# A run-through that orders the engines' steps, with eight numbers of its durations changed

## The reference

```
def peer(xn, wq, k1, k2, u_tab, v_tab):          # 8 heads, 128 x 128 experts
    q = xn @ wq                                   # two halves of 128 per head
    v1, i1 = top_k(q1 . k1, 16); v2, i2 = top_k(q2 . k2, 16)
    sv, ci = top_k(v1[:, None] + v2[None, :], 16) # 16 experts per head and token
    experts = e1 * 128 + e2                       # 128 per token
    hid = gelu(einsum("td,tkd->tk", xn, u_tab[experts]))
    return einsum("tk,tkd->td", softmax(sv) * hid, v_tab[experts])
```

## Time and profile before

| | |
|---|---|
| time, median of 3 runs | 2053.2 us (2052.7 to 2058.16) |
| the profiled execution's own time | 2048.43 us |
| its span, first to last instruction | 2046.6 us |
| TensorE's mean granted clock | 0.914 of 2.4 GHz |
| busy: PE, DVE, ACT, POOL | 81%, 69%, 40%, 30% |
| moved by DMA | 770.09 MB, mean 376 GB/s |

### The profile page before, as it was taken

How to read it: one execution, slowest core, us unless ns; L and a number is a source line. 1 busy time by engine, 2 the same in 40 slices (tenths; PEclk the granted TensorE clock), 3 DMA queues, 4 the chain that set the end, 5 groups by cost and what they waited for, 6 DMA issues and landing times.

```text
span 2046.6 us, 20781 instructions
## 1 busy us (share of the span) xinstructions
PE 1666.4 (81%) x6676; PEld 963.3 (47%) x6676; DVE 1406.5 (69%) x3607; ACT 817.2 (40%) x2072; POOL 610.9 (30%) x516
## 2 busy tenths in 40 slices
PE   8999989998889888886778877876887887756555
PEld 4449856583477464472326434532553463221111
DVE  4324327468776478866887876888887688877776
ACT  2423213433488236423444553333455324432222
POOL 0000000021422324523443343244425324454542
PEclk9999989899989999898889889988998899887878
DMA  9686868469999999999999999999999999999997
GB/s 391 211 312 237 298 227 279 170 222 388 386 419 419 420 418 407 420 418 407 420 420 419 419 419 420 399 420 420 419 420 412 416 354 419 419 420 420 421 420 306
DMA packets 108382, 770.09 MB, mean 376 GB/s; under 512 B 12144, under 2 KB 12656, under 8 KB 16368
## 3 DMA queue, kind: packets, MB, share of 16 engines
q0 software_dynamic: 73728, 536.90, 63.7%
q1 hardware_dynamic: 34544, 231.85, 29.4%
HBM read 767.65 MB, written 1.05 MB: 376 GB/s over the span
## 4 chain that ended last, share of the span: by engine, by line
PE 39%; DMA 37%; DVE 10%; issue 8%; ACT 3%; POOL 3%; SPq 0%; DVEq 0%; POOLq 0%
DMA arena<-in_peer_dram,eidx 10%; DMA ring<-in_peer_dram,eidx 10%; PE psum L1109 9%; DMA ring<-in_slabs_dram 9%; PE psum L745 8%; PE psum L768 8%; PE psum L954 6%; DMA kv<-in_peer_dram,eidx 5%; DMA early<-in_peer_dram,eidx 3%; PE psum L971 3%; DVE x L2023 2%; DVE arena L2013 1%; POOL arena L2165 1%; POOL ring L2165 1%; PE psum L786 1%
## 5 line engine op out<-in xcount | busy, mean ns | idle before, releaser
L2165 POOL DMA_INDIRECT arena<-in_peer_dram,eidx x203 | 244.8, 1206 | 832.5 <-DVE eidx L1885 440.2
L1109 PE MATMUL psum<-arena,diag 128*128 128x512 f32 x548 | 307.5, 694 | 109.1 <-ACT diag L1441 108.6
L1431 ACT ACTIVATE wexp<-wexp 128x1 f32<-128x1 f32 x512 | 103.2, 202 | 676.2 <-DVE wexp L2013 674.5
L2013 DVE CUSTOM_DVE_ANT_0 arena<-arena,osb 128x1024 f32<-128x1024 f32 x203 | 247.0, 1221 | 79.6 <-DMA arena<-in_peer_dram,eidx 76.8
L1109 PE MATMUL psum<-ring,diag 128*128 128x512 f32 x428 | 225.8, 661 | 61.4 <-ACT diag L1441 60.8
L2165 POOL DMA_INDIRECT ring<-in_peer_dram,eidx x155 | 185.0, 1193 | 295.8 <-PE psum L1109 234.3
L745 PE MATMUL psum<-ring,hT 128*128 128x512 f32 x560 | 258.6, 613 | 16.7 <-DMA ring<-in_slabs_dram 14.6
L1109 PEld LDWEIGHTS psum<-arena,diag 128*128 128x128 f32 x548 | 111.7, 216 | 269.6 <-ACT diag L1441 160.2
L2013 DVE CUSTOM_DVE_ANT_0 ring<-ring,osb 128x1024 f32<-128x1024 f32 x155 | 188.4, 1221 | 58.9 <-DMA ring<-in_peer_dram,eidx 57.0
L1109 PE MATMUL psum<-kv,diag 128*128 128x512 f32 x284 | 158.8, 688 | 53.3 <-ACT diag L1441 52.9
L954 PE MATMUL psum<-hT,ring 128*128 128x130 f32 x1408 | 168.0, 282 | 12.6 <-DMA ring<-in_slabs_dram 11.8
(11 more groups left out here) (328 smaller groups left out, 2131.0 us busy)
## 6 DMA issues: line engine op xcount, KB each, us to landing
ring<-in_slabs_dram SPq DMA_DIRECT2D x200, 1024.0 KB, 4.9
ring<-in_slabs_dram SPq DMA_DIRECT2D x8, 768.0 KB, 4.1
kept<-in_slabs_dram SPq DMA_DIRECT2D x4, 1024.0 KB
arena<-in_peer_dram,eidx POOLq DMA_INDIRECT x203
ring<-in_peer_dram,eidx POOLq DMA_INDIRECT x155
ring<-in_slabs_dram SPq DMA_DIRECT2D x4, 512.0 KB
kk<-in_keys_dram SPq DMA_DIRECT2D x2, 1024.0 KB, 8.9
kv<-in_peer_dram,eidx POOLq DMA_INDIRECT x105
```

The source lines that it names most:

```text
L1109: ins = pe.matmul(bank(b), diags_of(n), pair(slot_of[n])[:, 1024 + 512 * h:1536 + 512 * h], start=(k == 0), stop=(k == 127))
L1431: act.activation(wn, wn, ACT.Gelu_apprx_tanh).then_inc(*up("gelu", n))
L2013: v.tensor_tensor_reduce(out=row, in0=row, in1=row_y[t], scale=1.0, scalar=0.0, op0=ALU.mult, op1=ALU.add, accum_out=wexp[:, c:c + 1]).the ...
L2165: pool.indirect_dma_start(pair(i), None, tables, bass.IndirectOffsetOnAxis(ap=eidx[:, 128 * t + k:128 * t + k + 1], axis=0)).then_inc(sig. ...
```

## The change

Eight numbers of the run-through are set lower: the durations of a dot, a weight, a down on PE and a down on DVE, the floor and the constant part of a matmul's, and the constant parts of those of DVE's instructions.

```
-... T_DOT, T_WEIGHT, T_DIAG, T_TENSOR, T_VECTOR ... = ... 1.35, 0.55, 0.42, 2.1, 1.35 ...
+... T_DOT, T_WEIGHT, T_DIAG, T_TENSOR, T_VECTOR ... = ... 1.16, 0.52, 0.42, 1.8, 1.21 ...
     def matmul(self, out, lhsT, rhs, **k):
-        return self.run(max(0.232, 0.02 + 0.00166 * wide(rhs)) * (0.75 if lhsT.shape[0] <= 64 else 1.0))
+        return self.run(max(0.225, 0.01 + 0.00166 * wide(rhs)) * (0.75 if lhsT.shape[0] <= 64 else 1.0))
...
     def _vector(self, out, src, *a, **k):
-        return self.run(0.2 + 0.00107 * max(wide(out), wide(src)))
+        return self.run(0.12 + 0.00107 * max(wide(out), wide(src)))
...
     def tensor_tensor_reduce(self, out, in0, **k):
-        return self.run(0.28 + 0.00107 * wide(in0))
+        return self.run(0.2 + 0.00107 * wide(in0))
```

More of the change, by code:

```diff
@@ L29 @@
 ADD = ((0, 2), (6, 7), (0, 1), (6, 7))
-T_MB, T_SEEN, T_ISSUE, T_DOT, T_WEIGHT, T_DIAG, T_TENSOR, T_VECTOR, T_TABLE, T_HOP, T_KEEP, T_LEAN, T_AHEAD, T_LATE, T_PACE, T_SHRINK, T_FLIGHT, T_END, T_HEAD, T_FRESH, T_SCARCE, T_SOON, T_QUERY, T_ATT = 2.5, 2.0, 1.15, 1.35, 0.55, 0.42, 2.1, 1.35, 1.28, 0.12, 6, -2.0, 14, 0.0, 3.0, 0, 8, 0, 20, 0.5, 0, 10, 57, 62
+T_MB, T_SEEN, T_ISSUE, T_DOT, T_WEIGHT, T_DIAG, T_TENSOR, T_VECTOR, T_TABLE, T_HOP, T_KEEP, T_LEAN, T_AHEAD, T_LATE, T_PACE, T_SHRINK, T_FLIGHT, T_END, T_HEAD, T_FRESH, T_SCARCE, T_SOON, T_QUERY, T_ATT = 2.5, 2.0, 1.15, 1.16, 0.52, 0.42, 1.8, 1.21, 1.28, 0.12, 6, -2.0, 14, 0.0, 3.0, 0, 8, 0, 20, 0.5, 0, 10, 57, 62
 ENGINES = ("PE", "DVE", "ACT")
```

## The result

The changed kernel takes 2067.53 us (median of 4 runs, 2064.74 to 2070.72). The kernel before took 2054.71 us (2052.7 to 2058.16) in the runs beside it. The ratio is 1.0066, 95% interval 1.0046 to 1.0086: the change makes the kernel about 13 us slower. The prediction said 2048 us with a range of 2036 to 2064; the measured time lies outside of it. The profiled execution took 2070.72 us, its span is 2068.6. Three executions of the kernels with halved instructions further down, at 2581 to 2920 us, were in a slow state and are left out of every number.

A forecast was written before the change was run, and what follows sets the result against it. DMA, full at 420 GB/s, was taken as the bound. Terms of -6.7 us (440 to 530) and +1.5 (530 to 1660), the others 0, gave -5.2: 2053.2 to 2048 us, range 2036 to 2064.

The forecast's parts named there:

- What bounds the kernel: Whole span: DMA, full at 420 GB/s, needs 1833.5 of 2046.6 us; in the other 213 us it was not filled.
- Part 1: 0 to 440 us, up to the first gather: order swaps change nothing, 0, with 3 us to either side.
- Part 2: 440 to 530 us: earlier gathers close the 7.7 us hole, -6.7 us; between 0 and at most 12 of gain.
- the 8 us that I had named: Sign for 470 to 530 us: POOL never waits over 8 us there after the change.
- Part 3: 530 to 1660 us: stages packed into fewer pairs raise PE's share to 0.91; +1.5 us, bounds -16.7 and +24.
- M11's hole: End of M11, near 1500 us: the old hole of 8.1 us stays, some 150 us earlier, at 6 to 10 us.
- "about 18 us" of queue: Gather's issue to landing near the end: 20.52 us, transfer 2.5; a down may be about 18 us late before DMA notices.
- PE late in the stages: Rival: ends of M01 and M10 get holes of 8.1 us each, +9.5, 2063; 2071 if M11's doubles; chance 0.13.
- Its sign: Pairs 40 to 80, end of B1 and start of M01: a stretch with PE over 95% busy and DMA under 400.
- Part 4: Fourth tile, some 190 pairs with nearly all downs on PE: 2.44 us each, under 2.5 a pair, so 0.
- the rival of a PE alone at a low clock: Last 190 pairs: downs average over 2.5 us and every pair lags; +18 us, 2066 or 2071; chance 0.10.
- Part 5: The end: the last two downs stay on PE at 3.94 us; 0, at worst +3.6.

The follow-up runs named there:

- Halved dots: Changed kernel, same streams, each dot over 512 of its 1024 columns: 2045.21 us; the same edit in the kernel before: 2050.36 us.
- halved downs: Changed kernel, same streams, each down on PE one matmul instead of two except a tile's first and last: 2061.36 and 2057.69 us in two runs.
- the versions with a margin: Changed kernel with DVE's constants back at 0.2 and 0.28: 2041.23 us; with T_KEEP 8 for 6: 2040.18 us; with both: 2040.57 us.
- T_KEEP at 8: Changed kernel, T_KEEP 8 for 6, so dots and downs go ahead of steps with two pairs fewer landed: 2040.18 us, ratio 0.9942.

## Why the prediction was wrong, step by step

**What bounds the kernel** held: DMA at 420 GB/s, and each loss is time in which it was not filled. The sum over stretches closes within 1 us for both kernels.

**Part 1**, no change up to the first gather, was off by more than its own bound of 3 us: the first gather begins at 434.83 us, not 440.62, which is more than the 5 us that I had named as a sign of being wrong, and the stretch to 440 gained 3.1 us. I had counted the instructions ahead of it and taken a swap of single steps for nothing.

**Part 2** was right in place and sign, with a gain of 10.3 for 6.7. The hole of 7.7 us shrank to 1.8 (401 GB/s), the ramp before it from 4.9 to 0.6, which I had as the outer bound only. The downs of PE after the first came within 1 us of where I had put them (472.01 to 498.76), but 20 gathers were issued by 500 us, where I worked out 24 and before had 15. POOL waited twice for longer than the 8 us that I had named, 8.57 us before 474 and 13.23 before 515. The second wait follows 17.8 us of DVE without a dot, which looks like the mechanism of part 3 in small.

**Part 3 is the step that failed**: "I take +1.5 for the denser packing", bounds -16.7 and +24; it was +35.9. M11's hole, named at 6 to 10 us, was 19.7. The working behind it counted PE's share of each 20 to 40 pairs against DMA's and found 0.91 at most. DVE's was never counted. Its cover of "about 18 us" of queue was taken for a late down and put beside PE's work alone, though a late dot delays the same place. In fact the same packing that shortened the stages put DVE's searches, index arithmetic and mixers among fewer pairs: L rose from 11, 9 and 13 us in M01, M10 and M11 to 21, 20 and 20. Halved dots, which take work from DVE alone, give 22 us back. The row was there to see the earlier trace rows: DVE was busy 27.27 and 27.99 of 30 us at 1300 and 1660, the two stretches of before that had a hole, and PE 22.48 and 24.30. I read them for their GB/s and named PE from POOL's waits.

The rival "PE late in the stages" (0.13) had the right stages, M01 and M10, and a time near the measured one, 2063 to 2071. Its reason, "it decides where PE's share passes 1", holds for neither M10 nor M11: halved downs leave those holes nearly as they are. For M01 it was partly right. Its sign, pairs 40 to 80 with PE over 95% busy and DMA under 400 GB/s, came for 20 us (19.51 of 20 busy, 330 GB/s, at pairs 66 to 70), and halved downs take half of that hole away. M01's hole is not at that stage's end, where the rival had it, but in its middle.

**Part 4** was right. The 340 us from 1690 on stay at 420 GB/s, and the rival of a PE alone at a low clock fell. One line of PE's timeline and one stretch of the changed kernel near the end:

```profile
1934.10 1.98 PE L1109 MATMUL psum<-arena,diag 128*128 128x512 f32 x4 [0.51 <-ACT diag L1441]
```

```profile
1900.00:2000.00 100.00, 78.23 (x159) 1.00 1.01 420
```

Every down takes 1.98 us at a granted clock of 1.00, with gaps of 0.51 us, as the forecast had it (0.5 us, over 0.85). Before, it was 58.73 us for 20 downs at 0.74; now 78.23 for 40. The reading behind it was looser than it sounded: of the downs in the earlier trace rows the slowest, 3.78 us, follows 1.21 us of idle time and not 3. The Trainium skill's advice to run matmuls back to back (Perfetto Trace Analysis, "Matmul Optimizations") did not make this pattern of single downs a bad one here.

**Part 5** held: the end lost 12.7 us, and 13.8 before.

Parts 1 and 2 together measured -13.4 us; taken from 2053 that is 2040, about what the versions with a margin reach (2040 to 2041), though each of them gets there by a sum of its own. These beat both kernels, so with T_KEEP at 8 the same change is a gain of about 12 us.

## What to carry to other kernels

When a planner's durations are set to the measured ones, the excess in the old numbers may have been the only slack between its model and the chip: look for the queue it protected, and give that slack a number of its own. Count every engine's share of each stretch against the transfer that bounds it, not only the busiest engine's, and trust the row of a hole (who is busy 19 of 20 us in it) over the name that ends a wait, which is only the last link. To find the late engine, keep the order and shrink one engine's instruction, then compare hole by hole: the total mixes places with different causes, as M01 and M11 here.

## What the runs showed of the hardware

Halving the downs in the fourth tile, where PE has nothing else, freed almost nothing of PE. The stretch of the changed kernel with halved downs, to be held against the 78.23 us at 1.00 above, and lines of its timeline:

```profile
1900.00:2000.00 100.00, 74.11 (x81) 0.62 1.01 420
```

```profile
1923.17 1.13 PE L1109 MATMUL psum<-arena,diag 128*128 128x512 f32 x2 [0.63 <-ACT diag L1441]
1925.66 2.07 PE L1109 MATMUL psum<-kv,diag 128*128 128x512 f32 x2 [1.37 <-ACT diag L1441]
...
1943.12 2.08 PE L1109 MATMUL psum<-ring,diag 128*128 128x512 f32 x2 [0.42 <-ACT diag L1441]
```

A down of one matmul took 1.12 to 2.08 us there, 1.85 on average, and one of two matmuls 1.98 in the changed kernel. The granted clock of the stretch was 0.62, a mean of the two levels, 1.2 and 2.4 GHz; a quick down (1.13 us) is followed by 1.37 us of idle time and then by downs of 2.07 us. With whole downs the clock was 1.00. I had expected the clock to suffer from 411 single downs 0.5 us apart, and it did not. By the rows of both kernels, PE's busy time in a stretch that it does not bound says little about the work in it.
